# A two-way recurrent scan inside one denoising layer: its operands brought to one fixed place each, its products in a new order

## The reference

```python
def rwkv_scan(s0, r, w, a, b, k, v):
    def step(s, inp):
        r_t, w_t, a_t, b_t, k_t, v_t = inp
        sa = jnp.einsum('bdhvk,bdhk->bdhv', s, a_t)
        s = s * w_t[..., None, :] + sa[..., None] * b_t[..., None, :] + v_t[..., None] * k_t[..., None, :]
        return s, jnp.einsum('bdhvk,bdhk->bdhv', s, r_t)
    s_fin, y = lax.scan(step, s0, (r, w, a, b, k, v))
    return y, s_fin
...
def layer(x, cond, lp, ctx=None):
    sh1, sc1, g1, sh2, sc2, g2 = modulation(cond, lp['w_ada'], lp['b_ada'])
    h = rmsnorm(x, lp['norm1_g']) * (1 + sc1) + sh1
    z = h @ lp['w_in']
...
    mixed = jax.nn.sigmoid(ga) * (y_a @ lp['w_out_a']) + jax.nn.sigmoid(gb) * (merge_heads(y_b) @ lp['w_out_b'])
    x = x + g1 * (mixed @ lp['w_out'])
    h2 = rmsnorm(x, lp['norm2_g']) * (1 + sc2) + sh2
    x = x + g2 * conv_ffn(h2, lp)
```

## Time and profile before

| | us |
|---|---|
| median of 3 runs (lowest to highest) | 2658.68 (2656.91 to 2662.21) |
| profiled execution | 2655.93 |
| its span, first to last instruction | 2654.0 |
| PE busy / PEld busy | 2427.3 / 1997.5 |
| DVE busy / ACT busy / POOL busy | 1352.5 / 699.4 / 656.4 |
| mean granted TensorE clock | 0.972 of full |

### The profile page before, as it was taken

The page is one execution under the profiler, slowest core; times in us unless marked ns, Lnnn a source line. Parts: engine busy times, 40 slices in busy tenths (PEclk is TensorE's granted clock), DMA queues, the critical chain, the costliest instruction groups (busy, mean ns, idle before and its releaser), DMA issues.

```text
span 2654.0 us, 50075 instructions
## 1 busy us (share of the span) xinstructions
PE 2427.3 (91%) x21498; PEld 1997.5 (75%) x21498; DVE 1352.5 (51%) x2117; ACT 699.4 (26%) x1159; POOL 656.4 (25%) x283
## 2 busy tenths in 40 slices
PE   2799999999999997777788999899999999999997
PEld 2677778787888786777754578788888888888886
DVE  7665656528697866444453332543433334333335
ACT  3272644735655431222210000310001000010002
POOL 0220120111111111111100035253344344444431
PEclk9899999999999998989988999899999999999999
DMA  6313111022566767223222320011110111111112
GB/s 241 99 51 109 49 60 59 27 107 70 168 178 185 205 173 238 83 88 100 72 90 99 107 96 32 16 42 38 41 41 32 41 40 40 33 40 41 36 37 87
DMA packets 176353, 225.09 MB, mean 85 GB/s; under 512 B 100898, under 2 KB 135842, under 8 KB 175266
## 3 DMA queue, kind: packets, MB, share of 16 engines
q1 hardware_dynamic: 176162, 222.19, 26.4%
HBM read 163.30 MB, written 57.02 MB: 83 GB/s over the span
## 4 chain that ended last, share of the span: by engine, by line
PE 79%; DVE 7%; issue 6%; ACT 2%; DMA 2%; SPq 2%; POOL 1%; DVEq 0%; ACTq 0%; POOLq 0%
PE PS L808 18%; PE PS L810 18%; PE PS L809 18%; PE PS L1249 5%; PE PS L917 3%; PE PS L931 2%; PE PS L1059 2%; SPq L658 2%; PE PS L889 2%; DVE buffer L1911 1%; DVE buffer L1910 1%; PE PS L903 1%; PE PS L960 1%; PE PS L891 1%; PE PS L1110 1%
## 5 line engine op out<-in xcount | busy, mean ns | idle before, releaser
L808 PE MATMUL PS<-buffer,buffer 128*128 128x512 f32 (+1 forms) x2784 | 1006.0, 361 | 19.8 <-POOL buffer L2167 8.3
L810 PE MATMUL PS<-buffer,buffer 128*128 128x512 f32 (+1 forms) x2784 | 997.4, 358 | 0.0
L809 PE MATMUL PS<-buffer,buffer 128*128 128x512 f32 (+1 forms) x2784 | 997.2, 358 | 0.0
L808 PEld LDWEIGHTS PS<-buffer,buffer 128*128 128x128 f32 x2784 | 526.7, 189 | 113.8 <-issue 17.9
L810 PEld LDWEIGHTS PS<-buffer,buffer 128*128 128x128 f32 x2784 | 526.8, 189 | 83.2
L809 PEld LDWEIGHTS PS<-buffer,buffer 128*128 128x128 f32 x2784 | 526.9, 189 | 81.9 <-issue 1.0
L2176 POOL TENSOR_TENSOR buffer<-buffer,buffer 128x1024 fp32r<-128x1024 f32 x76 | 183.9, 2420 | 856.5 <-PE PS L810 528.0
L2123 DVE SCALAR_TENSOR_TENSOR buffer<-PS,buffer,buffer 128x512 f32<-128x512 f32 (+1 forms) x264 | 158.4, 656 | 154.8 <-PE PS L810 154.8
L2177 POOL TENSOR_TENSOR buffer<-buffer,buffer 128x1024 fp32r<-128x1024 f32 x76 | 193.4, 2545 | 6.0
L2099 DVE TENSOR_SCALAR buffer<-buffer,buffer 128x1281 f32<-128x1281 f32 x22 | 34.5, 1568 | 291.7 <-ACT buffer L1680 291.7
L1680 ACT ACTIVATE buffer<-PS 128x512 f32<-128x512 f32 (+1 forms) x66 | 30.0, 530 | 513.6 <-PE PS L810 513.6
(11 more groups left out here) (209 smaller groups left out, 2916.2 us busy)
## 6 DMA issues: line engine op xcount, KB each, us to landing
buffer<-in_w_up SPq DMA_DIRECT2D x44, 512.0 KB, 3.4
buffer<-in_w_in SPq DMA_DIRECT2D x42, 512.0 KB, 5.1
ops_kept<-buffer SPq DMA_DIRECT2D x40, 512.0 KB, 5.7
buffer<-ops_kept SPq DMA_DIRECT2D x40, 512.0 KB, 4.3
buffer<-in_w_ada SPq DMA_DIRECT2D x32, 512.0 KB, 7.0
buffer<-in_w_down SPq DMA_DIRECT2D x22, 512.0 KB, 3.4
buffer<-in_x SPq DMA_DIRECT2D x20, 512.0 KB, 10.1
gates_kept<-buffer SPq DMA_DIRECT2D x16, 640.0 KB, 5.7
```

Of the source, the lines that this page charges most:

```text
L808: mm(out, w_hi, x_hi, start=start, stop=False)
L809: mm(out, w_hi, x_lo, start=False, stop=False)
L810: return mm(out, w_lo, x_hi, start=False, stop=stop)
```

## The change

The three slots go. Each operand has one place: A and R in `FX`, B and K in `FBK`, V in `FV`, and the inverses land by 16 DMAs of 32 partitions directly as zero-padded 64-wide blocks in `DX` (cleared once by POOL, whose `expand` is gone). ACT copies `FX` to `FY`, which the products with the state read. R is multiplied by r already in the tile stage (DVE, from r reloaded into `RS` by four more DMAs per unit), and the chunk-end decays are kept there (`PEND`). The units move three slots later; the last batch is solved by DVE in pairs 0 to 7 of the scan, four rows each, and stored at pair 9. The three whole loads of r, k and v move to pairs 3, 5 and 7. The state has one place, and the context's final state is turned after the last pair. The waits of x tiles go by pairs of tiles. All 20 pairs stay written out on PE.

```diff
-        UNIT_SLOT = [6 + 2 * u for u in range(NG_UNITS)]
+        UNIT_SLOT = [9 + 2 * u for u in range(NG_UNITS)]
...
-        SOLVE_SLOT = [(12 + 4 * b, 14 + 4 * b) if b < NBATCH - 1 else (28, 29) for b in range(NBATCH)]
+        SOLVE_SLOT = [(15 + 4 * b, 17 + 4 * b) for b in range(NBATCH - 1)]
...
+            def load_grams(i):
+
+                if i >= 1:
+                    sp.wait_ge(fy_ready, i)
+                    sp.wait_ge(gk_done, i)
                 sp.wait_ge(ops_out, 128 * (i // 4 + 1))
                 for d in range(2):
+                    sp.dma_start(FX[:, 2 * d:2 * d + 2].rearrange("p a j t -> p (a j t)"),
+                                 dram["ops_kept"][d, :, chunk_at(d, i) // C, 0:2 * NP * C]).then_inc(fx_in, 16)
...
+            def load_solved(i):
+
+                if i >= 1:
+                    sp.wait_ge(q_done, i)
+                else:
+                    sp.wait_ge(cleared, 4)
+                sp.wait_ge(solved_out, 256 * (i // 4 + 1))
+                for d in range(2):
                     n = chunk_at(d, i) // C
...
+                    for q in range(4):
+                        dst = DX[HB * q:HB * q + HB, :, d * NP:(d + 1) * NP, HB * (q % 2):HB * (q % 2) + HB]
+                        for kind in range(2):
+                            sp.dma_start(dst[:, kind], dram["solved_kept"][d, HB * q:HB * q + HB, kind, n * NP * HB:(n + 1) * NP * HB]
+                                         .rearrange("s (j t) -> s j t", t=HB)).then_inc(dx_in, 16)
...
+                if t - 1 in UNIT_SLOT:
+                    load_reads((t - 1 - UNIT_SLOT[0]) // 2)
...
+            load_solved(0)
             for i in range(1, NC):
-                load_pair(i)
-                if i == 2:
-                    store_solved(NBATCH - 1)
+                load_grams(i)
+                load_keys_b(i)
+                load_values(i)
+                load_solved(i)
...
+                if i in (3, 5, 7):
+                    n = (i - 3) // 2
+                    sp.dma_start(rkv[:, 4 * n:4 * n + 4, :], kept[:, 4 * n:4 * n + 4, :]).then_inc(state_in, 16)
+                if i == 9:
+                    store_solved(NBATCH - 1)
...
+            def turn(i, after, twice, loads, blocks, first=False):
+
+                if not first:
+                    hold((rh_out, i), (q_out, i))
+                    products(6, Q, RH).then_inc(u_done, 1)
+                hold((fx_in, loads), (fbk_in, loads))
+                gram(0, 2).then_inc(gb_done, 1)
+                if not first:
+                    hold((u_out, i), (ys_done, i))
+                    outputs_of_tokens().then_inc(y_done, 1)
+                    state_update().then_inc(st_done, 1)
+                    hold((vt_out, i))
+                gram(1, 4).then_inc(gk_done, 1)
+                if not first:
+                    hold((y_out, twice), (fy_ready, i))
+                to_tokens(Y_BANK, 0, lambda j: FBK[:, 2 * (j // NP), j % NP, :])
+                to_tokens(Y_BANK, NP * C, lambda j: FBK[:, 2 * (j // NP) + 1, j % NP, :]).then_inc(bk_done, 1)
+                hold((far_out, after), (s_ready, after), (dx_in, blocks))
                 products(7, GB[:, 0], DX[:, 1]).then_inc(lz_done, 1)
...
+                hold((gk_out, after), (fv_in, loads))
+                to_tokens(TURN_BANK, 0, lambda j: FV[:, j, :]).then_inc(vt_done, 1)
+                hold((lz_ready, after))
                 products(7, Z, DX[:, 0]).then_inc(q_done, 1)
...
+                hold((gb_out, after), (fy_ready, after))
+                rhs_of_state().then_inc(rh_begun, 1)
+                hold((vt_out, after))
+                rhs_of_values(EVEN)
+                hold((rh_begun, after))
+                rhs_of_values(ODD).then_inc(rh_done, 1)
+                hold((bk_out, after))
+                outputs_of_state().then_inc(ys_done, 1)
...
+                V.step(tt(SG[:, 0], SG[:, 0], PX2, ALU.mult))
+                dve.wait_ge(rs_in, 64 * (u + 1))
+                for n in range(2):
+                    part = E[:, 1, n * NX // 2:(n + 1) * NX // 2, :]
+                    ins = tt(part, RS[n], part, ALU.mult)
+                    if n == 0:
+                        V.step(ins)
+                    else:
+                        ins.then_inc(keys_ready, 1)
```

More of the change, by code:

```diff
@@ L265, in build @@
         consts_in = sem("consts_in")
-        tile_moved = [sem(f"tile_moved{b}") for b in range(TB)]
+        tiles_moved = [sem(f"tiles_moved{b}") for b in range(TB // 2)]
         ada_in = [sem(f"ada_in{s}") for s in range(4)]
@@ L1103, in seq_state, with state_update @@
-            def seq_state(n):
-                out = two_banks(0)
-                for lhs, rhs, first in ((Bt, U, True), (Kt, Vt[:, n % 2], False)):
+                for j, k in zip(ODD, EVEN):
+                    one(k)
+                    ins = one(j)
+                return ins
+            def state_update():
+                for lhs, rhs, first in ((Bt, U, True), (Kt, Vt, False)):
                     for j in range(2 * NP):
@@ L1109, in seq_state @@
                             f, t = halves(j, h)
-                            ins = mm(out[f, j % 2, j // 2, :], lhs[t, j, :], rhs[t, j, :], start=first and j < 2, stop=not first,
+                            ins = mm(at_bank(STATE_BANK, j)[f], lhs[t, j, :], rhs[t, j, :], start=first and j < 2, stop=not first,
                                      skip_group_check=True)
-                ins.then_inc(st_done, 1)
-            def seq_rhs(n):
-                p = n % 2
-                out = two_banks(0)
-                def of_state(j):
+                return ins
@@ L1188, in _, with hold @@
-            for i in range(NC):
-                if i == 1:
-                    pe.wait_ge(si_out, 1)
-                if i == NC_CTX + 1:
-                    pe.wait_ge(fin_read, 1)
-                pe_pair(i)
-            seq_u(NC - 1)
-            pe.wait_ge(y_out, 2 * NC - 2)
+                        ins = mm(at_bank(RHS_BANK, j)[t], GK[t, 0, j, :], Vt[t, j, :], start=False, stop=True, skip_group_check=True)
+                return ins
+            def hold(*waits):
+                pe.wait_ge(consts_in, 48)
+                for sem, value in waits:
+                    pe.wait_ge(sem, value)
@@ new lines, in _ @@
+            pe.wait_ge(z_out, len(TILES))
+            pe.wait_ge(ms_copied, NG_UNITS)
+            pe.wait_ge(state_in, 32)
+            state_turned(6, lambda j: SI[:, j, :]).then_inc(st_turned, 1)
+            turn(0, 1, 0, 32, 256, first=True)
+            pe.wait_ge(st_read, 1)
+            for i in range(1, NC):
+                turn(i, i + 1, 2 * i, 32 * (i + 1), 256 * (i + 1))
+            pe.wait_ge(rh_out, NC)
+            pe.wait_ge(q_out, NC)
+            products(6, Q, RH).then_inc(u_done, 1)
```

413 lines of the change are left out of this document (172 added, 241 removed).

## The result

| | before | after |
|---|---|---|
| median, us (lowest to highest) | 2658.3 (2656.9 to 2662.2) | 2722.4 (2708.9 to 2734.7) |
| ratio | | 1.0237, 95% interval 1.0195 to 1.0279 |
| profiled execution: span, us | 2654.0 | 2720.6 |
| mean granted clock of TensorE | 0.972 | 0.965 |

A forecast was written before the change was run, and what follows sets the result against it. The prediction took the scan to go by how fast TensorE's instructions arrive, the tile stage by PE. Its terms 11 + 18 + 19 + 15 + 5 = +68 us gave 2727 us, range 2675 to 2785.

The forecast's parts named there:

- The tile stage: Tile stage: two more multiplications per unit and four loads of r ahead of SP's stores end it +11 us later; bounds 1.5, 16.
- The start of the scan: Last tile to first product with an inverse: SP's stores precede the first inverse loads, 33.3 against 15.2 us, +18 us.
- The pace of a pair: Scan: a pair takes 16.7 instead of 15.72 us, +19 us over nineteen pairs; bounds -6 and +40.
- at the middle it costs nothing: Scan, SP's queue: its cycle of 14.5 us, at 0.42 a `DX` load, stays below the pair's 16.7 us.
- the sign that SP bounds: Profile after, scan: PE's waits name DMAs into `DX` in most pairs.
- the rival with SP's queue: Scan: each `DX` load takes 0.60 us or more, cycle 17.8 to 19 us, 2748 to 2770 us in all; chance 0.17.
- the arrival of instructions: Scan, PE: instruction fetch sets the pair; 6.7 us of DMA work, 0.7 us delay for each, gives 17.5 us, 15.4 without small pieces.
- pace stays: Scan: smaller loads and pieces hold up instructions less or not at all; 15.4 to 15.7 us a pair, 2702 to 2708; chance 0.15.
- The three whole loads: Scan, pairs 3, 5 and 7: r, k and v loads each hold up 5.5 us of instructions, +15 us; bounds 4, 31.
- The stores at pair 9: Scan, pair 9: stores take SP for 12 us, partly covered by idle time, +5 us; bounds 0 and 10.
- The tail after the scan: Stages behind the scan: claimed to cost nothing.
- Faster: Scan: instruction gaps vanish, 12.6 us a pair, 2649 us in all; chance 0.08.

## Why the prediction was right, and where it was not

- **The tile stage, +11: right, the mechanism in the main.** It measured +10.8, and the four loads of r ahead of the 16 stores are its cause. The sum had 4.7 us in two rounds and 1.4 in the first, for the multiplications; all three rounds paid for the loads, 3.5, 3.1 and 5.1 us, and the multiplications cost nothing that shows, since without the loads the last tile ends where it did before (1014.1 and 1014.4 us). PE's waits for the keys came in two units, 5.1 us in all; as much again (5.6 us) was the wait for ACT's sigmoids, which the prediction did not name. The rest is the granted clock of 0.97 to 0.98 that came with these waits, where it had been 1.00 (columns as above):

```profile
830.00:900.00 70.00, 65.63 (x484) 52.97 (x483) 53.19 (x89) 32.92 (x51) 10.91 (x4) 0.98 0.72 189
900.00:960.00 60.00, 55.83 (x424) 45.27 (x423) 45.80 (x79) 25.87 (x39) 7.64 (x3) 0.97 0.75 207
960.00:1014.00 54.00, 52.13 (x352) 42.33 (x351) 37.94 (x59) 27.63 (x43) 8.40 (x3) 0.97 0.67 175
```

- **The start of the scan, +18: the mechanism right, the size 5 us too high.** The order of SP's queue it is; moved, the first product comes 15.7 us sooner. The mis-sized terms are small ones: half a solve 13.5 us instead of 15.3, the landing of the last load some 1.4 us instead of 3.1, the stores 11.6 instead of 12.6, against 0.8 us more for the 16 loads, and a last tile that ended 8.3 us after the last keys instead of 7.
- **The pace of a pair, 16.7 us: the number right by luck, its reason half wrong.** The step that failed is the one on SP, "at the middle it costs nothing". A load into `DX` costs SP 0.65 us in the scan, where 0.42 was interpolated from two rows of other shapes; that gives 10.4 us for 16, and PE waits for `DX` in 14 of the 20 pairs. The prediction had named this as the sign that SP bounds, and the rival with SP's queue (0.17) had the mechanism and put the price at 0.60 or more. The other step, on the arrival of instructions, erred the other way: it priced the small pieces at 0.7 us of delay for each us of DMA work, and the kernel in which POOL has half of the loads, with all the same pieces, runs 15.13 us with the same 3.4 us of "issue" as before, which is the "pace stays" of the rivals. Two errors met at 16.7. The rival's time (2748 to 2770) was too high: its cycle has 7.8 us beside the 16 loads, and it measured 6.5 (16.75 less the 10.25 us that the 16 loads take on average). Its own terms give 3.0 + 1.7 + 9.6 + 3.1 = 17.4 us at 0.60 a load, not the 17.8 of the prediction.
- **The three whole loads, +15: measured 5.9.** The mis-sized term is the 0.7 us of held-up instructions for each us of DMA work, again; the 1.5 us taken off for the load of before has no working in the sum. **The stores at pair 9, +5: measured 6.0.**
- **The tail after the scan, put at nothing: wrong, by 13.5 us.** Work was counted there, which indeed stayed, not the place of the code: 10.0 us are the FFN loop's. The group norm's 3.5 us are PE's busy time at a lower granted clock (its two parts, first before, then after):

```profile
1341.29:1369.49 28.20, 28.10 (x128) 18.74 (x129) 19.52 (x28) 6.36 (x5) 0.00 (x0) 0.94 0.53 211
1369.49:1412.09 42.60, 26.29 (x60) 12.02 (x59) 21.22 (x29) 1.76 (x4) 0.00 (x0) 0.67 0.00 0
```

```profile
1394.37:1424.55 30.18, 30.09 (x129) 20.72 (x129) 19.52 (x28) 6.94 (x6) 0.00 (x0) 0.87 0.56 213
1424.55:1468.65 44.10, 27.78 (x59) 12.76 (x59) 21.23 (x29) 1.87 (x4) 0.00 (x0) 0.65 0.00 1
```

  PE is busy for 57.9 us instead of 54.4. The stage takes between 69.0 and 76.7 us in the traces of all the kernels, though none changes its work, so this part of the difference is no fixed cost of the change.
- **Faster**, the case in which the gaps vanish, did not happen, for a reason that the kernels with a loop make plain: fixed places alone shorten no program. The loop that they allow is worth 79 us.

Sum by stage: 10.8 + 13.2 + 29.0 + 3.5 + 10.0 = 66.5 us against 68. The total is so near by luck: an overestimate of 15 us (start and scan) met 13.5 us that were not foreseen.

## What to carry to other kernels

Where an engine waits for "issue" in a straight program, as here, what repaired it was fewer distinct instructions, not fewer bytes of data: bringing operands to fixed places paid only when the loop that it allows was written. A queue that issues many small DMAs in order is a chain like any other: count its issues per turn at the price that they have in that stage, and look at what stands ahead of the first load that somebody waits for. And when a change lengthens a long program, look at loops far behind it, since their place moves.

## What the runs showed of the hardware

- The issue of one and the same DMA (32 rows of four 128 B pieces) costs SP 0.47 us beside a TensorE that runs a loop, and 0.65 us beside one that runs a written-out program; on POOL it is 0.54 us beside either.
- TensorE gets through the same pair (480 matmuls and as many weight loads) in 11.69 us from a loop (granted clock 0.98) and in 15.1 us written out (1.00), with POOL's half of the loads in both and no wait for data in these pairs. The Trainium skill, "Runtime: NRT & Kernel Launch", Instruction fetch mechanics, calls the cost of a border between blocks of instructions mostly hidden; the 3.4 us speak against it here.
- A written-out stretch of TensorE's program shows as packets of 16 KB in an instruction queue, 27 in seven pairs; a loop of 980 instructions shows none.
- The program before the FFN loop being 139 instructions longer costs 1.7 to 2.7 us in each of four turns of it, in the changed kernel and in the kernel before with the loop shifted.
- The changed kernel's executions lie 26 us apart, those of each of the twelve other kernels 3 to 12 us; the cause was not pursued.
